# Hybrid encoder step: where the token gather and the scatter products of an expert job stand in the stream of weights

## The reference

```python
def moe(h, w_router, b_router, w1, w3, w2):
    logits = jnp.einsum('...d,de->...e', h, w_router).astype(jnp.float32) + b_router.astype(jnp.float32)
    top_v, top_i = lax.top_k(logits, TOP_K)
    top_w = jax.nn.softmax(top_v, axis=-1)
    combine = jnp.einsum('...k,...ke->...e', top_w, jax.nn.one_hot(top_i, N_EXPERTS, dtype=jnp.float32))
    y = None
    for e in range(N_EXPERTS):
        term = combine[..., e:e + 1].astype(h.dtype) * swiglu(h, w1[e], w3[e], w2[e])
        y = term if y is None else y + term
    return y
```

## Time and profile before

| what | value |
|---|---|
| median of three runs | 1971.55 us |
| the profiled execution, its own time | 1977.98 us |
| its span in the profile | 1976.2 us |
| PE busy | 1882.6 us (95%) |
| DVE busy | 1440.9 us (73%) |
| ACT busy | 1170.9 us (59%) |
| expert part, from the first gather to the last add to `x` | 858.9 to 1958.6 us of the span |

### The profile page before, as it was taken

How to read it: one execution, slowest core, us unless ns; L and a number is a source line. 1 busy time by engine, 2 the same in 40 slices (tenths; PEclk the granted TensorE clock), 3 DMA queues, 4 the chain that set the end, 5 groups by cost and what they waited for, 6 DMA issues and landing times.

```text
span 1976.2 us, 31336 instructions
## 1 busy us (share of the span) xinstructions
PE 1882.6 (95%) x10698; PEld 1653.7 (84%) x10698; DVE 1440.9 (73%) x1909; ACT 1170.9 (59%) x1522; POOL 19.7 (1%) x39
## 2 busy tenths in 40 slices
PE   7999998999899999889999999999999999999996
PEld 6999998999799999768878778778788787787785
DVE  5563565666655645459979979789799799798896
ACT  4453434333436344348868768678688587686784
POOL 1000000000000000000000000000000000000000
PEclk8999999999999999979999999999999999999999
DMA  7444543444344344329969969879799699698792
GB/s 281 142 161 147 180 162 110 169 152 174 126 162 142 112 146 167 132 87 373 363 240 373 365 236 374 307 291 368 262 361 375 231 373 371 232 372 330 290 371 85
DMA packets 67991, 478.95 MB, mean 242 GB/s; under 512 B 7840, under 2 KB 8864, under 8 KB 10704
## 3 DMA queue, kind: packets, MB, share of 16 engines
q1 hardware_dynamic: 65168, 467.82, 63.4%
q0 software_dynamic: 2608, 10.08, 1.5%
q10 hardware_dynamic: 144, 0.04, 0.0%
HBM read 474.23 MB, written 3.69 MB: 242 GB/s over the span
## 4 chain that ended last, share of the span: by engine, by line
issue 67%; PE 29%; DVE 2%; ACT 1%; DMA 0%; POOL 0%; SPq 0%; ACTq 0%; POOLq 0%; DVEq 0%
PE psum L1584 9%; PE psum L1586 9%; PE psum L1585 9%; DVE h L976 1%; DMA ring<-in_w_in 0%; PE psum L1464 0%; PE psum L1463 0%; DVE rstd L973 0%; DVE w_lo L986 0%; PE psum L1483 0%; ACT w_hi L686 0%; PE psum L1453 0%; DVE attn L1154 0%; PE psum L1525 0%; ACT L716 0%
## 5 line engine op out<-in xcount | busy, mean ns | idle before, releaser
L1338 DVE TENSOR_TENSOR w_lo<-ring,w_hi 128x1024 fp32r<-128x1024 f32 x448 | 543.4, 1224 | 71.5 <-ACT w_hi L873 47.0
L873 ACT ACTIVATE w_hi<-ring 128x1024 fp32r<-128x1024 f32 x448 | 476.1, 1065 | 116.6 <-PE psum L1684 83.5
L986 DVE TENSOR_TENSOR w_lo<-ring,w_hi 128x1024 fp32r<-128x1024 f32 x218 | 266.5, 1224 | 268.1 <-ACT w_hi L686 268.1
L686 ACT ACTIVATE w_hi<-ring 128x1024 fp32r<-128x1024 f32 x218 | 230.9, 1061 | 380.2 <-PE psum L1586 378.5
L1584 PE MATMUL psum<-h_hi,w_hi 128*128 128x288 f32 x1312 | 395.9, 302 | 33.7 <-DVE h_lo L992 22.9
L1585 PE MATMUL psum<-h_lo,w_hi 128*128 128x288 f32 x1312 | 390.8, 298 | 0.0
L1586 PE MATMUL psum<-h_hi,w_lo 128*128 128x288 f32 x1312 | 389.4, 297 | 0.0
L1682 PE MATMUL psum<-w_hi,h_hi 128*128 128x512 f32 x896 | 365.0, 407 | 0.8 <-issue 0.2
L1684 PE MATMUL psum<-w_hi,h_lo 128*128 128x512 f32 x896 | 354.5, 396 | 0.0
L1683 PE MATMUL psum<-w_lo,h_hi 128*128 128x512 f32 x896 | 353.8, 395 | 0.0
L1338 DVE TENSOR_TENSOR w_lo<-spare,w_hi 128x1024 fp32r<-128x1024 f32 x224 | 274.0, 1225 | 24.3 <-ACT w_hi L873 6.0
(11 more groups left out here) (230 smaller groups left out, 1959.5 us busy)
## 6 DMA issues: line engine op xcount, KB each, us to landing
ring<-in_e_w SPq DMA_DIRECT2D x224, 1024.0 KB, 4.9
spare<-in_e_w SPq DMA_DIRECT2D x112, 1024.0 KB, 4.8
ring<-in_w_in SPq DMA_DIRECT2D x56, 1024.0 KB, 4.9
ring<-in_w SPq DMA_DIRECT2D x33, 1024.0 KB, 4.8
ring<-in_w_branch SPq DMA_DIRECT2D x12, 1024.0 KB, 4.8
ring<-in_w_out SPq DMA_DIRECT2D x8, 1024.0 KB, 4.8
bias<-in_bias_t POOLq DMA_DIRECT2D x2, 1024.0 KB, 9.9
x<-in_x_t SPq DMA_DIRECT2D x4, 288.0 KB, 3.8
```

Source lines behind the costliest of these rows:

```text
L686: nc.scalar.activation(dst, src, ACT.Copy).then_inc(rounded, 1)
L873: nc.scalar.activation(w_hi[buf][:, :], expert_ring[s][:, half * CHUNK_W:(half + 1) * CHUNK_W], ACT.Copy).then_inc(rounded, 1)
L986: nc.vector.tensor_tensor(low, src, high.bitcast(f32), ALU.subtract).then_inc(split, 1)
L1338: nc.vector.tensor_tensor(w_lo[buf][:, :], expert_ring[s][:, half * CHUNK_W:(half + 1) * CHUNK_W], w_hi[buf][:, :].bitcast(f32), ALU.subtr ...
```

## The change

All jobs run in one order. A turn is now the two units of a pair, a job has seven turns, and `unit_down` of a job's last unit comes behind `unit_rows` of the next job's first unit, as within a job. The turns 0, 1 and 6 are written out, and a loop runs over the four between. The job before the loop of jobs and the last job are written out as well; the weights in HBM are rolled so that the order of use stays the order of loads.

The gather of the next job's tokens moves ahead of a job's last unit: it stands behind the transposes of unit 13 of 14. It is now in float32r, from a high and a low half of the token rows (`h_tok_hi`, `h_tok_lo`, made once ahead of the first job): 48 products of 128x128 into four banks. ACT copies the high result to `he_hi`, and DVE the low one to `he_lo`, when the last unit's rows are done.

The sums of a job are split to `y_hi` and `y_lo` and weighted by `slot_w` behind the next job's first unit. The eight scatter products, now eight pairs of float32r products, stand together behind the transposes of the next job's second unit, in two banks by turns: pair j waits until DVE has added pair j - 2. DVE's eight adds stand behind its last step of that unit. The one-hot matrix is transposed and the slot weights are picked once a job, behind its second turn (`turn_spread`). The products with a zero column go; the first product of a job clears the sums. The banks are fixed by purpose.

```diff
-TURNS = UNITS // 2 - 1
+TURNS = UNITS // 2
+TURN_CHUNKS = 12
...
+PEELED = 2
...
+        GATED, TURNED, SPARE, SUMS = (0, 1), (2, 3), (4, 5), (6, 7)
+        GATHER_HI, GATHER_LO = SPARE, (GATED[0], TURNED[0])
...
+            def sums_high():
+                act.wait_ge(chunk_used, turns.chunk(5))
+                act.wait_ge(slot_w_ready, turns.value(0 if turns.turn == 0 else 1, 1))
+                for hf in range(2):
+                    nc.scalar.activation(y_hi[:, hf * 512:(hf + 1) * 512], psum[:, SUMS[hf], :], ACT.Copy,
+                                         scale=slot_w[:, 0:1]).then_inc(y_hi_ready, 1)
...
+            def turn_work(t, last=False):
+                turns.turn = t
+                if not (turns.first and t == 0):
+                    round_chunks(4, 5)
+                round_chunks(6)
+                silu_unit(0)
+                round_chunks(7, 8, 9)
+                if t == 0 and not turns.first:
+                    sums_high()
+                hidden_high(0)
+                round_chunks(10, 11)
+                if not last:
+                    round_chunks(12)
+                silu_unit(1)
+                if t == TURNS - 1 and not last:
+                    gathered_high(1)
+                if not last:
+                    round_chunks(13, 14, 15)
+                hidden_high(1)
...
+            def gathered_low(hf, after):
+                dve.wait_ge(gathered, turns.value(4 * after + hf + 3, 4))
+                if after:
+                    dve.wait_ge(chunk_used, turns.chunk(9))
+                nc.vector.tensor_copy(he_lo[:, 4 * hf:4 * hf + 4, :].rearrange("p a b -> p (a b)"), psum[:, GATHER_LO[hf], :]
+                                      ).then_inc(he_lo_ready, 1)
...
+            def sums_low():
+                for hf in range(2):
+                    dve.wait_ge(y_hi_ready, turns.value((0 if turns.turn == 0 else 2) + hf - 1, 2))
+                    cols = slice(hf * 512, (hf + 1) * 512)
+                    nc.vector.scalar_tensor_tensor(out=y_lo[:, cols], in0=psum[:, SUMS[hf], :], scalar=slot_w[:, 0:1],
+                                                   in1=y_hi[:, cols].bitcast(f32), op0=ALU.mult, op1=ALU.subtract
+                                                   ).then_inc(y_lo_ready, 1)
...
+            def add_rows(*rows):
+                back = 1 if turns.turn < TURNS else 0
+                for j in rows:
+                    dve.wait_ge(scattered, turns.value(j + 1 - DT * back, DT))
+                    dve.wait_ge(x_ready, turns.value(MIXER_SUMS + j - DT * back, DT))
+                    nc.vector.tensor_tensor(x[:, j, :], x[:, j, :], psum[:, SPARE[j % 2], 0:TOK], ALU.add).then_inc(x_ready, 1)
...
+            def turned_spread():
+                dve.wait_ge(spread_turned, turns.value(1, 1))
+                nc.vector.tensor_copy(spread_t, psum[:, SPARE[0], 0:TOK]).then_inc(spread_t_ready, 1)
+                nc.vector.tensor_copy(slot_w[:, :], psum[:, SPARE[0], TOK:TOK + 1]).then_inc(slot_w_ready, 1)
...
+            def turn_work(t, e, following=None, last=False):
+                turns.turn = t
+                boundary = not turns.first
+                if not (turns.first and t == 0):
+                    low_chunks(4, 5)
+                low_chunks(6)
+                silu_times_g(0)
+                low_chunks(7, 8, 9)
+                if t == 0:
+                    if boundary:
+                        sums_low()
+                    nc.vector.tensor_copy(wsel[:, :], weight[:, :, bass.ds(e, 1)].rearrange("p n o -> p (n o)")
+                                          ).then_inc(wsel_ready, 1)
+                hidden_low(0)
+                low_chunks(10, 11)
+                if not last:
+                    low_chunks(12)
+                if t == TURNS - 1 and not last:
+                    gathered_low(0, 1)
+                silu_times_g(1)
+                if t == TURNS - 1 and not last:
+                    gathered_low(1, 1)
+                if not last:
+                    low_chunks(13)
+                if not last:
+                    low_chunks(14, 15)
+                hidden_low(1)
+                if t == 0 and boundary:
+                    add_rows(*range(DT))
+                if t == 1:
+                    turned_spread()
+                    if following:
+                        hot_rows(*following)
...
+                    dve.wait_ge(htok_high, 2 * n + hf + 1)
+                    cols = slice(hf * 512, (hf + 1) * 512)
+                    nc.vector.tensor_tensor(h_tok_lo[0:rows, n, cols], bank(("htok", n, hf), rows, 512),
+                                            h_tok_hi[0:rows, n, cols].bitcast(f32), ALU.subtract).then_inc(htok_low, 1)
...
+            def gather(after):
+                pe.wait_ge(spread_ready, turns.value(3 * (after + 1), 3))
+                if after:
+                    pe.wait_ge(spread_t_ready, turns.value(1, 1))
+                    pe.wait_ge(slot_w_ready, turns.value(1, 1))
+                    pe.wait_ge(x_ready, turns.value(MIXER_SUMS, DT))
+                for source, banks in ((h_tok_hi, GATHER_HI), (h_tok_lo, GATHER_LO)):
+                    for hf in range(2):
+                        if after and source is h_tok_lo:
+                            pe.wait_ge(*((e_prod_ready, turns.unit(0)), (e_lo_ready, turns.unit(0)))[hf])
+                        for j in range(4):
+                            at = (4 * hf + j) * P
+                            for n, (t0, rows) in enumerate(TILES):
+                                ins = nc.tensor.matmul(psum[:, banks[hf], j * P:(j + 1) * P], source[0:rows, n, at:at + P],
+                                                       spread[0:rows, n, :], start=(n == 0), stop=(n == 2))
+                        ins.then_inc(gathered, 1)
...
+            def scatter(*rows):
+                back = 1 if turns.turn < TURNS else 0
+                if rows[0] == 0:
+                    pe.wait_ge(y_hi_ready, turns.value(2 - 2 * back, 2))
+                    pe.wait_ge(y_lo_ready, turns.value(2 - 2 * back, 2))
+                for j in rows:
+                    if j >= 2:
+                        pe.wait_ge(x_ready, turns.value(MIXER_SUMS + j - 1 - DT * back, DT))
+                    out, cols = psum[:, SPARE[j % 2], 0:TOK], slice(j * P, (j + 1) * P)
+                    nc.tensor.matmul(out, y_hi[:, cols], spread_t, start=True, stop=False)
+                    nc.tensor.matmul(out, y_lo[:, cols], spread_t, start=False, stop=True).then_inc(scattered, 1)
...
+            def turn_spread():
+                pe.wait_ge(wsel_ready, turns.value(1, 1))
+                pe.wait_ge(x_ready, turns.value(MIXER_SUMS, DT))
+                plain = spread.bitcast(f32)
+                for n, (t0, rows) in enumerate(TILES):
+                    nc.tensor.transpose(psum[:, SPARE[0], t0:t0 + rows], plain[0:rows, n, :], ident[0:rows, 0:rows])
+                for n, (t0, rows) in enumerate(TILES):
+                    ins = nc.tensor.matmul(psum[:, SPARE[0], TOK:TOK + 1], plain[0:rows, n, :], wsel[0:rows, n:n + 1],
+                                           start=(n == 0), stop=(n == 2))
+                ins.then_inc(spread_turned, 1)
...
+            def turn_work(t, last=False):
+                turns.turn = t
+                boundary = not turns.first
+                unit_rows(0)
+                if boundary or t:
+                    unit_down(4, 1, last=(t == 0))
+                turn_hidden(0)
+                if t == TURNS - 1 and not last:
+                    gather(1)
+                unit_rows(1)
+                unit_down(10, 0, first=(t == 0))
+                turn_hidden(1)
+                if t == 0 and boundary:
+                    scatter(*range(DT))
+                if t == 1:
+                    turn_spread()
...
+            def job_work(last=False):
+                pe.wait_ge(he_hi_ready, turns.value(2, 2))
+                pe.wait_ge(he_lo_ready, turns.value(2, 2))
+                for t in range(PEELED):
+                    turn_work(t)
+                with pe.Fori(0, TURNS - PEELED - 1) as i:
+                    turns.i = i
+                    turn_work(PEELED)
...
-                for hf in range(2):
-                    nc.tensor.matmul(psum[:, 6 + hf, :], zero_col[:, :], he_hi[0:1, 0:4, :], start=True, stop=False)
...
-                gather("gather", 1 if is_last else 4)
-                pe.wait_ge(ytok_ready, job * 2 + 2)
-                pe.wait_ge(spread_t_ready, job + 1)
-                for j in range(DT):
-                    take(("scatter", j))
-                    give(nc.tensor.matmul(bank(("scatter", j)), y_tok[:, j * P:(j + 1) * P], wspread_t, start=True, stop=True))
```

More of the change, by code:

```diff
@@ L171, in groups_out @@
     return [("y", u, j) for j in range(DT)]
-UNIT_AT = {"first": 0, "odd": 1, "next": 2, "last": UNITS - 1}
-CHUNKS_IN = {"first": 4, "odd": 8, "next": 14, "last": JOB_CHUNKS - 4}
 def counted(names):
```

(33 more changed lines are left out.)

528 lines of the change are left out of this document (200 added, 328 removed).

## The result

The changed kernel takes **2043.2 us** (median of 4 runs, 2041.4 to 2044.4) against 1970.3 for the kernel before on the same chip: ratio 1.0357, 95% interval 1.0319 to 1.0395. It is 3.6% slower where 1.4% faster was forecast. The profiled execution took 2042.87 us. The later runs fell on several chips; the kernel before took 1970.3 to 1977.8 us on them, so small differences are read from ratios or from lengths within a profile.

The account below looks back on a forecast made before the run. PE was taken as the bound, DVE and DMA close behind. A change of jobs falls from 18.9 to 14.9 us, seven times 4.0; with start and last job 28.3 saved, giving 1943 us against 1971.55, range 1922 to 1970.

Parts of the forecast that it names:

- the gather's 0.12 us a product: Gather: 48 float32r products of 128 columns at 0.12 us, taken from six transposes, 5.8 us a job.
- The 0.176 us of an f32 pass: Old gather: 8.44 us over 48 passes; as the short products' price it would make the new gather 8.4 us.
- The upper bound: Gather: at most 48 x 0.23 = 10.9 us, since no one-pass product in the trace is dearer.
- The clock term: Behind the scatter's pause: one 3.4 us stretch at 0.51 clock a job costs 1.7 us, bounds 0 and 3.4.
- The rest of the sum: Change of jobs: gather 5.8, scatter 6.3, `turn_spread` 1.1 and clock 1.7 make 14.9 us against 18.9.
- The rounds: Scatter: each bank goes from DVE's add to PE's products and back, 1.1 us for two adds.
- The start: Ahead of the first job: rows start near 868.5 us instead of after 869.4, 0.9 us saved.
- The profile's offset: Whole kernel: the median of the runs lies 6.4 us below the profiled execution, so 1949.7 becomes 1943 us.
- Short products no cheaper than f32 passes: Rival, gather: float32r products cost 0.176 us, 18.4 us more, 1961.6; at 0.23, 1979. Chance 0.13.
- The code rival: PE's longer job loop doesn't fit, three code pieces a job are fetched again: up to 103 us, 2046. Chance 0.07.
- DVE did not fall behind: Rival: half of DVE's extra lumps show, 2 us a change, time 1956. Chance 0.12, shared with a second clock stretch.
- Pause hidden: Rival, scatter: adds come as soon as the pairs, so it costs 2.1 us, time 1914. Chance 0.04.

Follow-up runs that it names:

- pad: The changed kernel with the gather's third token tile (32 rows) filled up to 128 rows with zeros: 1965.7 us, ratio 0.9945 to the kernel before.
- pad_adds: The changed kernel with the padded gather, scatter in one place, and DVE's eight adds moved ahead of its last low parts: 1944.4 us, ratio 0.9845.
- f32g: The changed kernel with the kernel before's float32 gather at the new place, low part made by subtraction: 1987.2 us, ratio 1.0069.
- Series B: 39 accumulating float32r products, all of 128 rows, added behind PE's last product of the changed kernel: 0.11 us a product; whole run 2099.3 us.
- before_pad: The kernel before, with only its float32 gather's third tile filled up to 128 rows: 1949.3 us, ratio 0.9860.
- micro: The changed kernel plus series of 40 float32r products at six widths, 128 to 384 columns, behind PE's last product: 2089.2 us, a single run.
- f32pad_dist: The changed kernel with a float32 gather padded to 128 rows by zeroed one-hot rows, and the scatter in four places: 1918.0 us, ratio 0.9689.

## Why the prediction was wrong

- **The step that failed is the gather's 0.12 us a product.** It was taken from six transposes and meant to cover every product with 128 new weight columns. For 128 rows it was right (0.11). But a third of the gather's products have 32 rows, and with them a product costs 0.21 us at the full clock. The 0.176 us of an f32 pass was itself the sign: by their single records, of the six passes over pieces of 128, 128 and 32 rows two follow after 0.11 us, and the four from the entry into the 32-row piece to behind the way out of it after 0.20 to 0.21. I averaged over a pattern and called the mean the price of a pass.
- The upper bound held at the full clock: 48 x 0.212 = 10.2 us lies under 48 x 0.23 = 10.9. **What broke it was the clock**, which I had tied to pauses only. It fell without any pause, behind 5 us of gather, and took 13.2 - 10.2 = 3.0 us in the gather and some 2.3 in the last unit's rows (7.9 us instead of 5.6). The clock term was 0 to 3.4 us a job for the scatter alone. The price measured for all of it is 144.42 - 133.46 = 11.0 us a job; the spans of `pad` and of the changed kernel differ by 77.9 of the 100 us by which the time was missed.
- **The rest of the sum held in total, in part by luck.** With the gather padded a job takes 133.5 us; 132.8 was forecast. The gather was then 5.4 (5.8 forecast), the scatter with its waits 7.6 (6.3), `turn_spread` some 1.4 (1.1); the lower clock inside the scatter is in its 7.6, and behind it 0 to 1.7 were left (1.7), so that the misses partly cancel. The idle time at the third pair was 2.85 us, forecast some 3. The rounds took 0.72 to 0.76 us a pair at the lower clock, where 1.1 for two was forecast; at the full clock, in `pad_adds`, two took 1.17 (1020.62 to 1021.79). The lower clock at the scatter lasted 3.4 to 6.8 us a job in all, 1.7 to 3.4 us lost; I took 1.7.
- **The start** was forecast 0.9 us earlier and came 8.1 later (877.53 instead of 869.4): the first gather ran wholly at the lower clock, 16.3 us, where it was forecast at 5.8. The tail cost 3.9 us more, forecast none.
- **The profile's offset** of 6.4 us did not carry over: the changed kernel's profiled execution lies 0.4 us from its median.
- **Rivals.** "Short products no cheaper than f32 passes" was nearest: it named the right term and gave it too small a size (0.176 us, or 0.23 at most, at the full clock). The float32r products were even dearer than f32 passes, because a split gather goes over and back 16 times at 0.29 us where the f32 gather does it 8 times at some 0.38 (8.44 less 5.4 us is 3.0). Even `f32g`, with 8.4 us of gather, took 1987 where that rival had 1961.6. Its jobs are 136.5 us long, forecast 132.8 + 2.6 = 135.4; start, last job and tail together are 19.7 us longer than in the kernel before (19.6 in the changed kernel), and 6.4 us are the offset. The code rival is dead: by the DMA view from 860 us on, instruction pieces are nine in all, not three a job:

```profile
q8 instruction: 9, 0.15, 0.1%
```

  DVE did not fall behind: the idle spots on `w_lo` show in no unit of the middle. "Pause hidden" did not come: the scatter cost 7.6 us and not 2.1.
- **A small error of the working** changes nothing: from 75.3 us of 80, DVE has 0.5 us to spare in 8.42, not 0.6.
- The Trainium skill (TensorE: Matmul & The Clock Gate, Back-to-back issue gap) has 81 ns a pair at 128 columns. Series B measured 111 ns for float32r with 128 rows, the gather 212; the page's figure is met by neither.

## What to carry to other kernels

Look at a group by shape before taking its mean as a price: where pieces of 128 and of 32 rows alternate, the going over costs nearly as much again as the products (0.29 us on 0.33 for three, at the full clock), and here it brought the lower clock with it. Fill the last piece up to 128 rows with zeros on one side, or keep pieces of equal rows together; here that alone made the kernel before 1.4% faster (`before_pad`). And work that is short for PE but depends on another engine pair by pair is spread over several steps, not put in one.

## What was not expected of the hardware

- Float32r products of 128, 192 and 240 columns all cost 0.11 us at 2.4 GHz, 256 columns 0.12 (`micro`). Two passes of float32 with 128 columns and 128 rows cost 0.11 each, the same as two float32r products (`f32pad_dist`).
- A round trip from 128 rows to 32 (or 64) and back adds 0.29 us to three products at 2.4 GHz, and at 1.2 GHz the three take 1.02 us (0.27, 0.35, 0.40).
- The granted clock fell under an unbroken row of products: in the mixtures, and behind 39 products of 32 rows at 0.11 us, while 39 products of 128 rows at the same distance kept it. The float32 gather alternates between 128 and 32 rows too, at 0.175 us a pass, and kept the full clock for its 8.4 us in `f32g`. What the cases in which it fell have in common, no run here separates; that the float32r mixture is what lowered it in the gather is shown by `pad` and `f32g`.
